# Five head stripes of an attention turned by the DMA crossbar instead of by TensorE

## The reference, cut to what matters

```python
q_b = jnp.einsum('bsr,rn->bsn', rms_norm_2(c_q, q_lat_g), w_uq).reshape(b_sz, s_len, H_B, D_HQK)
kv_b = jnp.einsum('bsr,rn->bsn', rms_norm_2(c_kv, kv_lat_g), w_ukv).reshape(b_sz, s_len, H_B, D_NOPE + D_VB)
k_nope, v_b = jnp.split(kv_b, [D_NOPE], axis=-1)
k_b = jnp.concatenate([k_nope, jnp.broadcast_to(k_r[:, :, None, :], (b_sz, s_len, H_B, D_ROPE))], axis=-1)
q_b = rms_norm_2(q_b, q_norm_g)
k_b = rms_norm_2(k_b, k_norm_g)
q_b = jnp.concatenate([q_b[..., :D_NOPE], apply_rope(q_b[..., D_NOPE:], cos, sin)], axis=-1)
k_b = jnp.concatenate([k_b[..., :D_NOPE], apply_rope(k_b[..., D_NOPE:], cos, sin)], axis=-1)
o_b = causal_attention(q_b, k_b, v_b).reshape(b_sz, s_len, D_B)
y_b = jnp.einsum('bsc,cd->bsd', o_b * jax.nn.silu(z_b), w_b)
```

## Time and profile before

| what | value |
|---|---|
| median of 3 runs | 2118.58 us (2118.26 to 2118.92) |
| the profiled execution's own time | 2118.28 us |
| its span | 2116.5 us |
| TensorE busy | 2106.2 us, 100% of the span |
| VectorE, ScalarE busy | 67%, 52% |
| granted TensorE clock | 1.0 |
| queue of the weight loads (q1) | 64.3% of 16 engines' span |

### The profile page before, as it was taken

The page is one execution under the profiler, slowest core; times in us unless marked ns, Lnnn a source line. Parts: engine busy times, 40 slices in busy tenths (PEclk is TensorE's granted clock), DMA queues, the critical chain, the costliest instruction groups (busy, mean ns, idle before and its releaser), DMA issues.

```text
span 2116.5 us, 27015 instructions
## 1 busy us (share of the span) xinstructions
PE 2106.2 (100%) x9588; PEld 1745.3 (82%) x9588; DVE 1417.7 (67%) x1944; ACT 1096.1 (52%) x1519; POOL 58.8 (3%) x70
## 2 busy tenths in 40 slices
PE   9999999999999999999999999999999999999999
PEld 7888887888888888888788888888888888888887
DVE  5999868665565655656777546666445866766763
ACT  6546666554444444444575545554444665564452
POOL 0011100000000000000000000000000000000000
PEclk9999999999999999999999999999999999999999
DMA  8565564766775776766467765556666775666985
GB/s 317 186 212 180 177 229 159 223 214 202 228 211 189 219 203 205 212 197 209 158 214 214 242 198 182 196 175 215 202 205 210 201 227 159 191 180 207 348 254 163
DMA packets 198772, 439.94 MB, mean 208 GB/s; under 512 B 93928, under 2 KB 94320, under 8 KB 198384
## 3 DMA queue, kind: packets, MB, share of 16 engines
q1 hardware_dynamic: 196608, 431.79, 64.3%
q0 software_dynamic: 1744, 6.29, 0.9%
q10 hardware_dynamic: 288, 0.14, 0.0%
HBM read 407.21 MB, written 10.49 MB: 197 GB/s over the span
## 4 chain that ended last, share of the span: by engine, by line
PE 96%; DVE 2%; issue 1%; ACT 1%; DMA 0%; POOL 0%; ACTq 0%; DVEq 0%
PE g L650 31%; PE g L652 31%; PE g L651 31%; DVE arena L1555 1%; PE s L629 1%; DVE wlo L1485 0%; PE s L826 0%; PE s L825 0%; DVE ta_lo L1662 0%; PE s L704 0%; PE s L689 0%; PE s L733 0%; PE s L833 0%; ACT whi L915 0%; DMA vc<-in_vec 0%
## 5 line engine op out<-in xcount | busy, mean ns | idle before, releaser
L1485 DVE TENSOR_TENSOR wlo<-raw,whi 128x1024 fp32r<-128x1024 f32 x732 | 887.7, 1220 | 520.7 <-ACT whi L915 519.0
L915 ACT ACTIVATE whi<-raw 128x1024 fp32r<-128x1024 f32 x732 | 768.8, 1057 | 694.1 <-PE g L652 627.2
L650 PE MATMUL g<-whi,ta_hi 128*128 128x512 f32 x1920 | 757.6, 395 | 4.6 <-DVE wlo L1477 1.6
L652 PE MATMUL g<-whi,ta_lo 128*128 128x512 f32 x1920 | 748.2, 390 | 0.0
L651 PE MATMUL g<-wlo,ta_hi 128*128 128x512 f32 x1920 | 747.4, 389 | 0.0
L650 PEld LDWEIGHTS g<-whi,ta_hi 128*128 128x128 f32 x1920 | 360.6, 188 | 80.9 <-issue 7.1
L652 PEld LDWEIGHTS g<-whi,ta_lo 128*128 128x128 f32 x1920 | 360.4, 188 | 76.3
L651 PEld LDWEIGHTS g<-wlo,ta_hi 128*128 128x128 f32 x1920 | 360.8, 188 | 71.7
L650 PE MATMUL g<-whi,tb_hi 128*128 128x512 f32 x1008 | 395.5, 392 | 0.0
L652 PE MATMUL g<-whi,tb_lo 128*128 128x512 f32 x1008 | 392.5, 389 | 0.0
L651 PE MATMUL g<-wlo,tb_hi 128*128 128x512 f32 x1008 | 392.3, 389 | 0.0
(11 more groups left out here) (239 smaller groups left out, 963.0 us busy)
## 6 DMA issues: line engine op xcount, KB each, us to landing
raw<-in_w_in SPq DMA_DIRECT2D x318, 512.0 KB, 4.1
raw<-in_w_up SPq DMA_DIRECT2D x128, 512.0 KB, 4.1
raw<-in_w_down SPq DMA_DIRECT2D x128, 512.0 KB, 4.0
raw<-in_w_out SPq DMA_DIRECT2D x64, 512.0 KB, 4.3
raw<-in_w_a SPq DMA_DIRECT2D x32, 512.0 KB, 4.3
raw<-in_w_b SPq DMA_DIRECT2D x32, 512.0 KB, 5.7
raw<-in_w_ukv SPq DMA_DIRECT2D x16, 512.0 KB, 3.8
raw<-in_w_uq SPq DMA_DIRECT2D x12, 512.0 KB, 3.7
```

The costliest lines, as they stand in the source:

```text
L650: e.matmul(o, xh, wh, start=first, stop=False)
L652: ins = e.matmul(o, xl, wh, start=False, stop=last)
L915: e.activation(whi[u % RING][:, 0:n], raw[u % RAW][:, 0:n], ACT.Copy).then_inc(s_hi, 1)
L1485: e.tensor_tensor(l, r, h.bitcast(F32), ALU.subtract).then_inc(s_lo, 1)
```

## The change

Five more stripes go by jobs. The turns of TensorE and the evictions of them go; the cuts, DMA transposes and joins come, each at a slot of its own. Four waits keep buffers apart: the sources and targets of the new jobs lie in `stage` buffers and in the arena where the values of the first half and the softmax buffers of a head lie. The job order becomes ... uq1, uk0, uk1, ao0, ao1, qr1, uq2, uq3, uk2, uk3, ao2, ao3.

Slots of the new steps: uk0 cut 1208, issue 1210, join 1219. qr1 cut 1263, issue 1265, join 1277. uq2 cut 1274, issue 1276, join 1287. uq3 cut 1278, issue 1281, join 1295. uk2 cut 1300, issue 1302, join 1311.

```diff
@@ job table
+        CBM["uk", 0] = (ar(17408, 1024), flat[1], None)
         CBM["uk", 1] = (ar(16384, 1024), flat[3], None)
         ao_job(0)
         ao_job(1)
+        CBM["qr", 1] = (ar(17408, 1024), flat[2], None)
+        for n in range(2):
+            CBM["uq", 2 + n] = (ar(16384 + 1024 * n, 1024), ar(11264 + 1024 * n, 1024), None)
+        CBM["uk", 2] = (ar(16384, 1024), ar(17408, 1024), None)
         CBM["uk", 3] = (flat[1], flat[3], None)
@@ pe: uqr_side, uqn_side and ukn_side go (and their entries in the table of banks)
-                    turn(b, SG[3], pair).then_inc(qr_t.sem, 1)
...
-                    turn(b, SG[k // 2], k % 2).then_inc(uq_t.sem, 1)
...
-                    turn(b, SG[2], k % 2).then_inc(uk_t.sem, 1)
@@ act: zb_side, gb_side
-                        q.wait_ge(*((w_cut, cut(("uq", 1))) if n == 1 else (uq_t, 4)))
+                        q.wait_ge(w_cut, cut(("uq", n)))
...
+                    if n == 1:
+                        q.wait_ge(uk_c, 2)
@@ act: qr_side, uq_side
-                for pair in range(2):
-                    yield E("uqr1") + 16 + 2 * pair
-                    q.wait_ge(qr_t, pair + 1)
-                    q.wait_ge(at_s, 8)
-                    e.activation(HQR[:, 2 * pair:2 * pair + 2, :], two(TBK["qr", pair]), ACT.Copy).then_inc(qr_c.sem, 1)
+                yield E("uqr1") + 26
+                q.wait_ge(at_s, 8)
+                join_heads(("qr", 1), qr_c)
...
-                for k in range(4):
-                    yield E(f"uqn1{k // 2}") + 2 + 2 * (k % 2)
-                    q.wait_ge(uq_t, k + 1)
+                for i in range(2):
+                    yield E(f"uqn1{i}") + (16, 20)[i]
                     q.wait_ge(at_s, 8)
-                    e.activation(HQT[:, 2 * k:2 * k + 2, :], two(TBK["uq", k]), ACT.Copy).then_inc(uq_c.sem, 1)
+                    join_heads(("uq", 2 + i), uq_c)
@@ act: ukn_side, key_side, uv_side
-                    q.wait_ge(*((qr_v, 1), (qr_c, 2), (qr_v, 2), (ao_l, 4))[i])
+                    q.wait_ge(*((qr_v, 1), (qr_c, 2), (qr_c, 4), (ao_l, 4))[i])
...
-                    for pair in range(2):
-                        yield E(f"ukn{hf}0") + 8 + 2 * pair
-                        q.wait_ge(uk_t, 2 * hf + pair + 1)
-                        q.wait_ge(*((ml_o, 8), (at_s, 8))[hf])
-                        e.activation(HKT[:, 2 * pair:2 * pair + 2, :], two(TBK["uk", 2 * hf + pair]), ACT.Copy).then_inc(uk_c, 1)
+                    yield E(f"ukn{hf}0") + 16
+                    q.wait_ge(*((ml_o, 8), (at_s, 8))[hf])
+                    join_heads(("uk", 2 * hf), uk_c)
...
+                        q.wait_ge(uq_c, 8)
@@ dve: uqr_side, uq_side, ukn_side, at_side, ao_side
-                    if hf == 0:
-                        yield E("uqr0") + 12
-                        q.wait_ge(qr_v, 1)
-                        cut_heads(("qr", 0), flat[3])
+                    yield E(f"uqr{hf}") + 12
+                    q.wait_ge(qr_v, hf + 1)
+                    if hf == 1:
+                        q.wait_ge(at_o, 8)
+                    cut_heads(("qr", hf), flat[3])
...
-                for i in range(2):
-                    yield E(f"uqn0{i}") + 3
+                for i in range(4):
+                    yield E(f"uqn{i // 2}{i % 2}") + 3
                     q.wait_ge(uq_r, i + 1)
-                    cut_heads(("uq", i), flat[i])
+                    if i >= 2:
+                        q.wait_ge(at_o, 8)
+                    cut_heads(("uq", i), flat[i % 2])
...
+                    if n == 0:
+                        yield E(st.name) + 5
+                        q.wait_ge(uk_m, i + 1)
+                        cut_heads(("uk", i), flat[2])
...
+                        if i >= 8:
+                            q.wait_ge(uk_c, 6)
...
-                        q.wait_ge(qr_t, 2)
+                        q.wait_ge(w_cut, cut(("qr", 1)))
@@ sync: turn_side
-                        yield E("uqr0") + 14
+                        yield E(f"uqr{n}") + 14
                     elif name == "uq":
                         yield E(f"uqn{n // 2}{n % 2}") + 5 + n % 2
+                        if n >= 2:
+                            q.wait_ge(at_o, 8)
                     elif name == "uk":
-                        yield E(f"ukn{n // 2}1") + 12
+                        yield E(f"ukn{n // 2}{n % 2}") + (7, 12)[n % 2]
+                        if n == 0:
+                            q.wait_ge(zb_c, 2)
```

More of the change, by code:

```diff
@@ L452, in two_blocks @@
         d_turn, w_cut, w_join = Later(d_gain0, 16), Later(upad, 1), Later(word_join, 0)
-        uq_t = Later(qk_t, 8)
-        qr_t = Later(qr_turn, 0)
         kr_t = Later(ln_t, 4)
-        uk_t = Later(ln2_t, 4)
         yt_t = Later(x_t, 32)
@@ L597, in two_blocks @@
         use += [(LNS[k], "ln", k) for k in range(8)]
-        use += [(E("uqr1") + 16 + 2 * k, "qr", k) for k in range(2)]
-        use += [(E(f"uqn1{k // 2}") + 2 + 2 * (k % 2), "uq", k) for k in range(4)]
-        use += [(E(f"ukn{k // 2}0") + 8 + 2 * (k % 2), "uk", k) for k in range(4)]
         use += [(E(f"ukn{k // 2}1") + 13 + k % 2, "kr", k) for k in range(4)]
@@ L782, in ml_side @@
                             e.matmul(b2[:, 0:258], s[:, 256:384], v[:, 1], start=False, stop=True).then_inc(ml_o, 1)
-            def uqr_side():
-                for pair in range(2):
-                    yield E("uqr1") + 16 + 2 * pair
-                    b = bank(TBK["qr", pair], (qr_c, 3 + pair))
-                    q.wait_ge(qr_v, 2)
-                    turn(b, SG[3], pair).then_inc(qr_t.sem, 1)
-            def uqn_side():
-                for k in range(4):
-                    yield E(f"uqn1{k // 2}") + 2 + 2 * (k % 2)
-                    b = bank(TBK["uq", k], (uq_c, 5 + k))
-                    q.wait_ge(uq_e, 3 + k // 2)
-                    turn(b, SG[k // 2], k % 2).then_inc(uq_t.sem, 1)
[L798 to L802, removed]
-                    turn(b, SG[2], k % 2).then_inc(uk_t.sem, 1)
             def kr_side():
@@ L851, in pe @@
             sides = [Side(g) for g in (u_side(), qk_side(), na_side(), ln_side(), norm_side(B1, X1),
-                                       norm_side(B2, X2), row_side(), ml_side(), uqr_side(), uqn_side(), ukn_side(), kr_side(),
+                                       norm_side(B2, X2), row_side(), ml_side(), kr_side(),
                                        at_side(), y_side())]
```

## The result

The changed kernel takes **2126.22 us** (median of 5 runs, 2124.84 to 2128.16), the kernel before 2118.58 (5 runs, 2118.26 to 2118.92). The ratio is **1.0037 [1.0025, 1.0048]**: slower by 7.6 us, 0.36%. The forecast was 2119.5 with a range to 2121.8, and the result lies above it. The profiled execution took 2126.9 us, with a span of 2125.1.

A forecast was written before the change was run, and what follows sets the result against it. TensorE, busy for all of the span, was taken as the bound. Turns -4.7 plus stalls 1.9, 1.7, 1.4 and 0.7 made +1.0 us, hence 2119.5 us, range 2113.8 to 2121.8.

The forecast's parts named there:

- Scores of the second half: stall 0.7: Behind uk2's job, join, split and two rope-key evictions, ready at 1889.8; TensorE wants the scores at 1889.1: 0.7 us.
- Unit 654: stall 1.4: VectorE's low half of unit 654, behind uq3's join and ukn10's eviction, ends at 1874.4, wanted at 1873.0: 1.4 us.
- First half: stall 0: uk0's job, join and the rope-key evictions end at 1736.1, before first scores at 1737.8: no stall, 1.6 us to spare.
- The turns, -4.7: Ten turns leave TensorE's queue at 0.47 us each: 4.7 us saved, 0.94 before the first scores, 3.76 after.
- the list of waits costed at nothing: at_o 8, uk_c 6, zb_c 2 and the w_cut in ao_side: waits for things long done, costed at nothing.
- Unit 643: stall 1.9: qr1's job holds load 641 on SP; VectorE's low half ends at 1841.4, TensorE wants it at 1839.5: 1.9 us.
- Unit 648: stall 1.7: uq3's job delays load 649, whose split precedes zb3's evictions, ending 1856.7; TensorE wants the banks at 1855.0: 1.7 us.
- That it could end slower: Rival: slow crossbar issues, up to 2.16 us, on SP's queue at qr1, uq3 and uk2; 2123.2 us, chance 0.08.
- the two slower rivals: Slow issues on SP's queue, 2123.2 us, chance 0.08; the crossbar as the bound, 2124.8 us, chance 0.02.
- The crossbar is no bound: Rival judged: a new job takes another 6.8 us to land, uk0's join 5.2 us beyond margin; 2124.8 us, chance 0.02.
- The bound on the stalls: Stalls of TensorE: 0 at least if loads land earlier, 9.3 us at most with the slowest issues seen.

The follow-up runs named there:

- experiment 7: The kernel of experiment 6 with uk1's job issued two slots earlier, ahead of load 616 in place of load 618; 2115.65 us, 0.9988.
- experiment 4: The changed kernel with qr1 issued and joined eight slots later, its job behind loads 641 to 644; 2123.8 us, 1.0023.
- experiment 6: The changed kernel with the last rope-key turn in bank 2, and qr1's issue and join and uq3's join eight slots later; 2116.54 us, 0.9990.
- experiment 10: The changed kernel with only uq3's join eight slots later, behind the evictions of ukn10 and ukn11; 2125.17 us in 4 runs, 1.0035.
- experiment 9: The kernel of experiment 7 with the scaling of ukn11 one slot later; 2116.07 us, 0.9988.
- experiment 5: The changed kernel with the last rope-key turn in PSUM bank 2 in place of bank 3; 2123.04 us, 1.0021.
- experiment 3: The changed kernel with uk2's join at slot 1314 in place of 1311, behind the two evictions of rope keys; 2125.69 us, 1.0035.
- experiment 8: The kernel of experiment 4 with uk2 turned by TensorE as before, the other four stripes by the crossbar; 2119.41 us, 1.0003.
- experiment 11: The kernel of experiment 9 with the joins of uk1 and uk3 eight slots later; 2114.34 us, 0.9980.

## Why the prediction was wrong, step by step

The steps that failed are three terms of the sum. "Scores of the second half: stall 0.7" took 4.9 us, since TensorE waited for a shared bank and then ran at half clock; "Unit 654: stall 1.4" took 3.1, mostly at unit 656, which the walk never looked at; "First half: stall 0" took 0.9. The other terms held within 0.4 us.

- **The turns, -4.7: right.** Taken out alone they gave 4.85.
- **"First half ... stall 0": wrong, 0.9 us.** The margin of uk0's own chain to the scores held. What failed is the list of waits costed at nothing: it holds the waits that the change adds and not an old wait for a job that the change pushes back. uk1 stands behind uk0 in a chain of jobs that go one by one, and experiment 7, with uk1's job issued earlier, has no wait there.
- **"Unit 643: stall 1.9": right,** 2.3 by the starts of the matmuls (2.03 as a wait). Load 641 and low 643 came at the times worked out, within 0.4 us of them, and experiment 4 removed the stall by moving the job that I had named.
- **"Unit 648: stall 1.7": right,** 1.6. zb3's evictions ended at 1856.9, as predicted (1856.7).
- **"Unit 654: stall 1.4": right in the cause, wrong in place and size.** The eviction of ukn10 behind uq3's join did make VectorE late (its squares start at 1862.39). But I ordered VectorE by due slots alone and missed that a generator gives its steps in its own order. Nothing stalled at 654. Low 655 ended when I had said (1876.9 against 1876.7), and 1.0 fell on it. Another 2.1 fell on 656, 3.1 together: behind low 655 I looked at no low half, and so at neither the scaling of ukn11 nor its root, which the squares pushed behind low 654 left uncovered. Experiments 6 and 10 took away the stall at 655 and half of that at 656, and experiment 9 the rest.
- **"Scores of the second half: stall 0.7": wrong by 4.2 us, the largest part.** The chain of job, join, split and evictions was right: the first eviction ended at 1888.6, against 1888.7 worked out. I let TensorE wait only for the second, at the scores. The table of banks gives both rope-key turns of this half bank 3, so TensorE waits for the first eviction already in front of the second turn, where nothing else can be done, 3.3 us. And after it the clock stood at half, 1.6 us. Neither was in the sum. Experiment 5 shows the bank's part: with the second turn in bank 2 the place cost nothing. What a fall of the clock adds shows at unit 643 as well: the place cost 2.3 us with a wait of 2.03 and the clock at full, 4.1 with a wait of 2.33 and the clock at half (experiment 10).
- **The rivals.** That it could end slower was right, its mechanism was not: four transposes of a job take 5.12 to 5.13 us of issue at all three places that it named, not 2.16 each. Slower jobs do occur (5.72 for uq2 here, 6.49 for qr1 in experiment 4), but none at those three places in the changed kernel. That the numbers of the two slower rivals, 2123.2 and 2124.8, lie nearer to the measured time is luck. The crossbar is no bound either: uk2's join starts 6.35 us after the first issue of its job (1877.40 to 1883.75), against the 6.8 of ao1's. Behind it, the Trainium skill (VectorE: DVE Perf Modes, The three transpose paths) lists 1309 ns for a 128x128 bf16 transpose by the crossbar; one by one, a stripe's sixteen blocks would take 20.9 us, an estimate from that page. The trace doesn't agree with that sum here either: uk2's sixteen took at most the 6.35 us.
- **The bound on the stalls** (9.3 at most) rested on slow issues alone. The measured 12.8 came from orders and a shared bank that my walk through the schedule didn't have; the range was too narrow for a hand-made schedule in which five jobs each touch three in-order engines. It even stopped short of its own bound: 2118.58 - 4.7 + 9.3 is 2123.2, and the range ended at 2121.8. (The forecast's terms add up to 2119.6, not 2119.5; that changes nothing.)

Open: why the clock falls after some waits of about two microseconds and not after others (below), and with it the exact size of the loss from run to run. Whether each of the three kinds of move in experiment 6 is needed was not tried one by one beyond experiments 4, 5 and 10.

## What to carry to other kernels

Work taken off the bound engine is gained only as far as the steps put in its place keep out of the way of what the bound engine needs next: here the same instructions gave +7.6 us or -4.1 us by their slots and one bank. Before giving such a change up, list the waits of the bound engine, and for each ask which new step stands in front of the late one on its engine; then move that step, and expect the next one in line to show. When predicting, walk every generator in its own order, every job behind a delayed job, and every bank or buffer that a delayed eviction holds.

## What the runs showed of the hardware

A wait of TensorE can cost more than itself. After the 3.29 us of waiting at 1888.64 the granted clock was 0.50 until 1892, and matmuls of 512 columns started 0.43 us apart instead of 0.22: 1.6 us on top. In the traces kept, from 1500 us on, the clock went to half within 0.9 us of the end of each of the six longest waits: 2.21 at unit 643 in experiment 3, 2.28 in experiment 8, 2.33 at 643 in experiment 10 (where the place cost 4.1 us in place of 2.3), and 3.03, 3.11 and 3.29 at the rope keys (experiments 10, 4 and the changed kernel). With shorter ones it went either way: it fell 0.6 and 1.5 us after waits of 1.85 (experiment 5) and 1.89 (experiment 3) at unit 656. It stayed at 1.00 after 1.84 there in experiment 4, after 1.87 and 2.03 in the changed kernel, and after 2.15 at 643 in experiment 5. So nearly the same wait at the same place ended differently.

The runs point the same way: the mean granted clock of the changed kernel is 0.998 in four of five and its times spread over 3.3 us; in experiment 11, with no wait above 0.4 us, it is 1.0 in ten of 11 and they spread over 1.1 us. That the clock makes the spread isn't shown: the one run of the changed kernel at 0.999 is its second slowest.

A DMA transpose holds the queue that issues it far longer than a plain load does: over the changed kernel's trace, SP was held 1.26 us by one transpose in the median and 0.33 us by one 512 KB load.
